# Expert selection cut into pieces, expert gates in full precision, input loaded ahead of the weights, and both norms of the first half pipelined on VectorE

## The chip, the cores and the metric

The kernel runs on one core of a Trainium2 chip. The metric is the device time of one execution in microseconds (us), the median of several runs. A core has five engines that run their own instruction streams and meet at semaphores: TensorE (PE) multiplies matrices, VectorE (DVE), ScalarE (ACT) and GpSimd (POOL) work on tiles in on-chip memory, and SyncE (SP) issues most transfers (DMAs). "PEld" is TensorE's loading of stationary operands.

## The reference

Two model halves run one after the other on 256 tokens of 2048 features, all in float32. Cut to what the change touches:

```python
# first half
h = rms_norm(x, mix_norm_g[l])            # first norm
proj = h @ w_in[l]                        # attention, an S5 scan and a gated merge follow
x = x + merged @ w_out[l]
h2 = rms_norm(x, ffn_norm_g[l])           # second norm
x = x + peer(h2, ...)                     # experts by product keys
# peer, for each of 256 tokens and 8 heads
q = (ht @ w_query).reshape(t_, PEER_HEADS, 2, PEER_HALF)
v1, i1 = lax.top_k(s1, 16)                # the 16 best of 128 keys, twice
v2, i2 = lax.top_k(s2, 16)
cand = v1[..., :, None] + v2[..., None, :]      # 256 sums of pairs
top_s, pos = lax.top_k(cand, 16)
idx = take_along_axis(cand_idx, pos, -1)  # 16 of 16384 experts
gate = jax.nn.softmax(top_s, axis=-1)
w = gate * gelu(u_sel . ht)               # u_sel: rows idx of expert_down
y = w @ v_sel                             # v_sel: rows idx of expert_up
```

The second half (a latent-attention layer and a grouped-query layer, with their norms) is not touched.

## The kernel before

**Products.** A float32 weight tile of 1 MB (128 rows x 2048) comes from HBM into a ring of slots. It is split into a high part `w_hi`, a rounded copy that TensorE takes as fp32r (ACT, `hi_split`, L371 to L380), and a remainder `w_lo = w - w_hi` (`lo_split`, L382 to L389, two halves of 1024 columns: half h = 0 and half h = 1). The activations are split alike into `h_hi` and `h_lo`. `dense` (L395 to L412) then does 16 blocks of three matmuls of 256 columns (hi x hi, lo x hi, hi x lo), 48 in all. It waits for `lo_done[1]` ahead of block 0 and for `lo_done[0]` ahead of block 8. As a rule POOL makes half 0 and DVE half 1. `w_hi` and `w_lo` are double, and a new `w_hi` waits until the tile two before is multiplied.

**Start.** SP issues the two halves of the input `X` (L453) and at once the weight tiles (L457), as many as there are free slots, seven at first. ACT's own queue brings vectors and constants (`vec`, `cst`), and ACT starts when they are in.

**Norms** (first norm ahead of the first weight tile, second norm ahead of the tiles `wq`). DVE takes a reciprocal (L1182) and makes `ht` in 16 steps, four to a quarter (L1185). ACT rounds each quarter to `h_hi` (L503). POOL subtracts for quarters 0 and 1 (`norm_lo`, L1017 to L1022), DVE for 2 and 3 (L1188 to L1193), after all 16 steps. TensorE waits for one quarter at blocks 0, 4, 8 and 12 of the first tile (`h_waits`, L1919).

**Stage "down0"** (64 weight tiles, `expert_down`): every token is multiplied with all 16384 experts, a tile giving 256 columns that ACT passes through GELU into `ab`. Meanwhile DVE selects experts (L1472 to L1490): for 8 heads and 2 token halves, 16 units in all, it makes 256 pair sums (L1480), takes the best 16 in two rounds (L1482, by `top16`), and looks up their two keys by comparing, multiplying and adding over 16 x 16 (L1486 to L1488). While DVE does that, in the first 4 * SELECT = 40 tiles, POOL makes both halves of `w_lo`. After tile 40 ACT waits for `sel_shifted`, takes the exponential of the selected scores (L697), DVE divides by the sums, and for the last 24 tiles DVE makes half 1 again.

**Stage "gates"** (32 groups of 8 tokens). TensorE turns the two keys and the weight so that the selected experts lie on partitions (L2117). DVE copies them to `kt` and `gp`, where `gp` is kept as a high and a low part (L1508, L1509). For each group DVE builds two one-hot tiles (`onehots`, L1525: `oh1` and `oh2`, shown in the trace by the buffers they live in, `w_lo` and `w_hi`). ACT multiplies `oh1` with the low part of the weights, eight tokens in eight instructions, and with the high part for the eighth (`gates_low`, L711 and L713). POOL does the high part of the other seven in one (`gates_high`, L1088). TensorE multiplies `oh2` by `g_hi` and by `g_lo` for each token (L2132, 16 fp32r matmuls of 128 columns), and the result, a 128 x 128 table of gates, is copied out by ACT (`gates_stage`, L722) and used by DVE to scale `ab` (L1531). A scaling of group n - 3 follows the one-hots of a group. Buffers are double.

**Order.** Every engine's order is as written in the code; loops `Fori` run on the engine.

## Time and profile before

| what | us |
|---|---|
| median of 3 runs | 4251.7 (4250.2 to 4260.3) |
| the profiled execution | 4263.7 |
| its span | 4261.7 |
| TensorE busy | 3990.8 (94%) |
| VectorE busy | 2483.0 (58%) |
| GpSimd busy | 1821.7 (43%) |
| ScalarE busy | 1667.3 (39%) |
| mean granted TensorE clock | 0.957 of full speed |

TensorE is busy nearly all the time, so work on another engine counts only where TensorE waits for it, or where TensorE runs at the lower of its two clocks. The chain of work that ended last goes through TensorE for 72% of the span, and through VectorE for 19%. The views that answer are those of single stretches (in a row of windows, "x" is the number of instructions, and the clock is the granted TensorE clock as a share of 2.4 GHz): the busy time by windows, the timeline, and the groups of one stage.

### The profile page before, as it was taken

The numbers are of one execution on the slowest core, as the hardware profiler recorded it, in microseconds if no ns is written. First come the engines' busy times: TensorE is split into PE (matmuls) and PEld (weight loads), VectorE is DVE, ScalarE is ACT, GpSimd is POOL, SyncE is SP. The second block draws the span as 40 slices with busy tenths as digits, with TensorE's granted clock in tenths as the row PEclk, the third lists the DMA queues.
The fourth block names the chain that finished last, engine by engine and source line by source line (L and its number), as shares of the span: only waits on it lengthen the run. The fifth ranks groups of instructions, "written<-read, shape, count | busy, mean of one in ns | idle before, by whom it ended". The sixth has DMA issues, their size and how long they took to land.

```text
span 4261.7 us, 73528 instructions
## 1 busy us (share of the span) xinstructions
PE 3990.8 (94%) x30180; PEld 3660.9 (86%) x30180; DVE 2483.0 (58%) x3055; ACT 1667.3 (39%) x2344; POOL 1821.7 (43%) x992
## 2 busy tenths in 40 slices
PE   7999998898998799999999999999999888979997
PEld 6776778798998799999999999999999556858877
DVE  5999965543799368777333577732221333657546
ACT  3222345543454466333444334422222122233574
POOL 4787843244487355444444444422222101233323
PEclk9999999999999876999999999999999899989999
DMA  5777763354555333555555555522222102213323
GB/s 203 307 298 293 276 242 134 117 192 159 178 188 177 130 126 107 187 187 187 215 213 204 193 190 178 185 101 99 98 98 91 58 30 99 89 60 138 119 91 137
DMA packets 132291, 679.30 MB, mean 159 GB/s; under 512 B 43665, under 2 KB 49937, under 8 KB 52369
## 3 DMA queue, kind: packets, MB, share of 16 engines
q1 hardware_dynamic: 89952, 641.77, 41.7%
q10 hardware_dynamic: 42160, 35.01, 2.5%
q8 instruction: 129, 2.11, 0.2%
q14 instruction: 50, 0.40, 0.0%
HBM read 664.15 MB, written 12.58 MB: 159 GB/s over the span
## 4 chain that ended last, share of the span: by engine, by line
PE 72%; DVE 19%; ACT 4%; issue 3%; POOL 1%; DMA 1%; DVEq 0%; ACTq 0%; POOLq 0%
PE banks L410 43%; PE banks L2150 16%; PE banks L2132 2%; PE banks L2270 1%; DVE w_lo L388 1%; DVE eq L1487 1%; DVE pq L1311 1%; PE banks L2062 1%; DVE banks L1301 1%; PE banks L2326 1%; ACT w_hi L380 1%; PE banks L2219 1%; DVE eq L1486 1%; DVE rq L1347 1%; PE banks L2218 1%
## 5 line engine op out<-in xcount | busy, mean ns | idle before, releaser
L388 POOL TENSOR_TENSOR w_lo<-ring,w_hi 128x1024 fp32r<-128x1024 f32 x533 | 1360.0, 2557 | 2224.2 <-ACT w_hi L380 2222.7
L410 PE MATMUL banks<-h_hi,w_hi 128*128 128x256 f32 (+1 forms) x6176 | 1660.2, 289 | 144.8 <-DVE w_lo L388 75.2
L410 PE MATMUL banks<-h_hi,w_lo 128*128 128x256 f32 (+1 forms) x6176 | 1637.4, 286 | 0.0
L410 PE MATMUL banks<-h_lo,w_hi 128*128 128x256 f32 (+1 forms) x6176 | 1637.2, 286 | 0.0
L380 ACT CAST w_hi<-ring 128x1024 fp32r<-128x1024 f32 x986 | 983.9, 1048 | 1065.5 <-PE banks L2150 459.0
L410 PEld LDWEIGHTS banks<-h_hi,w_hi 128*128 128x128 f32 x6176 | 1114.6, 190 | 215.8 <-issue 127.6
L410 PEld LDWEIGHTS banks<-h_lo,w_hi 128*128 128x128 f32 x6176 | 1117.8, 190 | 15.2
L410 PEld LDWEIGHTS banks<-h_hi,w_lo 128*128 128x128 f32 x6176 | 1114.3, 190 | 15.8 <-issue 0.5
L388 DVE TENSOR_TENSOR w_lo<-ring,w_hi 128x1024 fp32r<-128x1024 f32 x453 | 609.9, 1347 | 882.9 <-ACT w_hi L380 880.0
L2150 PE MATMUL banks<-wp_hi,w_hi 128*128 128x256 f32 x2048 | 577.0, 282 | 14.0 <-DVE wp_lo L1558 14.0
L2150 PE MATMUL banks<-wp_hi,w_lo 128*128 128x256 f32 x2048 | 575.1, 281 | 0.0
L2150 PE MATMUL banks<-wp_lo,w_hi 128*128 128x256 f32 x2048 | 575.1, 281 | 0.0
L2150 PEld LDWEIGHTS banks<-wp_hi,w_hi 128*128 128x128 f32 x2048 | 386.8, 189 | 16.4 <-issue 9.0
L2150 PEld LDWEIGHTS banks<-wp_lo,w_hi 128*128 128x128 f32 x2048 | 390.4, 191 | 0.0
L2150 PEld LDWEIGHTS banks<-wp_hi,w_lo 128*128 128x128 f32 x2048 | 388.2, 190 | 0.0
L1555 DVE TENSOR_SCALAR wp_hi<-ab 128x256 fp32r x128 | 314.3, 2456 | 0.7 <-DVE mods L1573 0.3
L683 ACT ACTIVATE ab<-banks 128x256 f32 (+1 forms) x128 | 49.3, 385 | 351.5 <-PE banks L410 351.4
L1042 POOL TENSOR_TENSOR cst<-tab 128x256 f32<-128x256 f32 x128 | 102.9, 804 | 73.6 <-DVE pq L1311 67.9
L2132 PE MATMUL banks<-g_hi,w_hi 128*128 128x128 f32 x256 | 107.2, 419 | 9.2 <-ACT g_hi L713 6.0
L2132 PE MATMUL banks<-g_lo,w_hi 128*128 128x128 f32 x256 | 106.3, 415 | 0.0
L1045 POOL TENSOR_TENSOR rot<-cst 128x256 f32<-128x256 f32 x128 | 97.8, 764 | 10.0
L1088 POOL TENSOR_TENSOR g_hi<-w_lo,gp 128x896 fp32r<-128x896 f32 x32 | 79.8, 2494 | 43.1 <-DVE w_lo L1525 43.1
(382 smaller groups left out, 4699.8 us busy)
## 6 DMA issues: line engine op xcount, KB each, us to landing
ring<-in_stream_dram SPq DMA_DIRECT2D x555, 1024.0 KB, 4.8
spare<-in_stream_dram SPq DMA_DIRECT2D x30, 1024.0 KB, 6.0
cst<-in_stream_dram SPq DMA_DIRECT2D x23, 1024.0 KB, 6.1
g_out<-stage ACTq DMA_DIRECT2D x32, 256.0 KB, 2.6
g_in<-g_out ACTq DMA_DIRECT2D x8, 1024.0 KB, 6.6
X<-in_x_in_dram SPq DMA_DIRECT2D x2, 1024.0 KB, 7.1
b_st<-in_ssm_b_dram ACTq DMA_DIRECT2D x8, 256.0 KB, 8.0
c_st<-in_ssm_c_dram ACTq DMA_DIRECT2D x8, 256.0 KB, 5.3
```

Source lines behind the costliest of these rows:

```text
L380: act.copy(w_hi[:, t.par, s], weights(t.slot)[:, s]).then_inc(hi_done, 1)
L388: eng.tensor_tensor(w_lo[:, t.par, s], weights(t.slot)[:, s], w_hi[:, t.par, s].bitcast(F32), ALU.subtract).then_inc(lo_done[h], 1)
L410: m = pe.matmul(bank(b, e - a, a), w[:, t.par, k], x(k)[:, a:e], start=first and a == 0, stop=last and e == n, skip_group_check=e - a < n)
L683: act.activation(ab[:, row], bank(t.bank(), T), ACT.Gelu).then_inc(acc_free[t.bank()], 1)
L1042: pool.tensor_tensor(rt[:, 0], A_(p0), B_(p1), ALU.mult)
L1045: pool.tensor_tensor(rot[:, u % 3, f], rt[:, 0], rt[:, 1], op).then_inc(S("rot_ready"), 1)
L1088: pool.tensor_tensor(g_hi[:, n % 2, 0:7], oh1[:, n % 2, 0:7].bitcast(F32), w, ALU.mult)\
L1301: m = dve.tensor_tensor_scan(scanned[:, z], dec, crossed[:, 1 - z], 0.0, ALU.mult, ALU.add)
L1311: m = dve.tensor_tensor(turned(u, pq[u % 3][:, f]), scanned, r[:, f:f + 1].to_broadcast([P, 2, T]), ALU.mult)
L1555: dve.tensor_scalar(wp_hi[:, j % 2], ab[:, i * 4 + j], 1.0, None, ALU.mult)\
L2132: m = pe.matmul(gate_banks(n)[:, t], oh2[:, n % 2, t], x[:, n % 2, t], start=(x is g_hi), stop=(x is g_lo))
L2150: m = pe.matmul(bank(k // 2, T, k % 2 * T), w[:, t.par, k], x[:, j % 2], start=(first and j == 0 and n == 0 and k % 2 == 0), stop=False, s ...
```

## The change

1. SP waits for the first half of `X` ahead of the first weight tile, and for the second half ahead of the second.
2. Both norms: POOL's part goes, and DVE makes all four `h_lo` quarters, quarter q - 1 behind the `ht` steps of quarter q. TensorE waits for DVE's count at all four places.
3. Selection: each of the 16 units is cut into three pieces (`pair_sums`, `second_half`, `keys_found`). One piece goes ahead of the two splits of a weight tile, tiles 4 to 51 of down0. DVE makes both halves of `w_lo` for all 64 tiles of down0, and POOL none. SELECT goes from 10 to 13: ACT takes the exponential after tile 52. The last two `sub_top` (L1455), which ran ahead of the loop, are spread over tiles 0 to 3.
4. Gates: `gp` is one float32 copy. ACT multiplies all eight tokens of `oh1` with it (eight instructions, `gw`), POOL does nothing, and TensorE does one full-precision matmul for each token in place of two fp32r ones.

The diff, cut to its core:

```diff
-SELECT = 10
+SELECT = 13
...
-        gp = place("gp", [P, 2, T], F32R, TA + 2 * K)
+        gp = place("gp", [P, T], F32, TA + 2 * K)
...
-        g_hi = place("g_hi", [P, 2, 8, P], F32R, TA + 4 * K)
-        g_lo = place("g_lo", [P, 2, 8, P], F32R, 64 * K + NVEC * 4 + CONST["nd"][0] * 4)
+        oh2 = place("oh2", [P, 2, 8, P], F32, 32 * K + idle * 8 * K)
+        oh1 = place("oh1", [P, 2, 8, P], F32, 48 * K + idle * 8 * K)
+        gw = place("gw", [P, 2, 8, P], F32, TA + 4 * K)
...
             for g in range(UNROLLED):
+                if g < 2:
+                    sp.wait_ge(S(f"x_in{g}"), 16)
...
                 for t in range(8):
-                    act.activation(g_lo[:, n % 2, t], oh1[:, n % 2, t].bitcast(F32), ACT.Copy,
-                                   scale=gp[:, 1, tokens(n, i, s, t, 1)].bitcast(F32))
-                act.activation(g_hi[:, n % 2, 7], oh1[:, n % 2, 7].bitcast(F32), ACT.Copy,
-                               scale=gp[:, 0, tokens(n, i, s, 7, 1)].bitcast(F32)).then_inc(S("g_lo_ready"), 1)
+                    m = act.activation(gw[:, n % 2, t], oh1[:, n % 2, t], ACT.Copy, scale=gp[:, tokens(n, i, s, t, 1)])
+                m.then_inc(S("gw_ready"), 1)
...
-            pool.wait_ge(lo_done[1], N0["down0"] + 1)
-            with pool.Fori(0, SELECT, 1) as i:
-                for j in range(4):
-                    for h in (1, 0):
-                        lo_split(pool, Tile("down0", j, i, 4).next(), h)
-            with pool.Fori(0, 16 - SELECT, 1) as i:
-                for j in range(4):
-                    lo_split(pool, Tile("down0", j, i, 4, skip=4 * SELECT).next(), 0)
-
-            def gates_high(n, i=None, s=0):
...
+            pool.wait_ge(lo_done[0], N0["up0"] + 1)
...
+            def norm(r, gain):
...
+                def low(q):
+                    c = slice(4 * q, 4 * q + 4)
+                    dve.wait_ge(S("h_hi_done"), 4 * r + q + 1)
+                    dve.tensor_tensor(h_lo[:, c], ht[:, c], h_hi[:, c].bitcast(F32), ALU.subtract)\
+                        .then_inc(S("h_dve"), 1)
+
                 for q in range(4):
                     for k in range(4 * q, 4 * q + 4):
                         m = dve.scalar_tensor_tensor(ht[:, k], X[:, k], V(gain, k), rs[:, 1], ALU.mult, ALU.mult)
                     m.then_inc(S("ht_ready"), 1)
+                    if q:
+                        low(q - 1)
+                low(3)
...
+            dve.wait_ge(lo_done[0], N0["down0"] + 1)
+            for n in range(64):
+                if n < 4:
+                    sub_top(14 + n // 2, n % 2)
+                elif n < 52:
+                    (pair_sums, second_half, keys_found)[(n - 4) % 3]((n - 4) // 6, (n - 4) // 3 % 2)
+                elif n == 53:
+                    weights_found()
+                if n == 51:
+                    dve.sem_inc(S("sel_shifted"), 1)
+                for h in (1, 0):
+                    lo_split(dve, Tile("down0", n).next(), h)
...
-            L(dve.tensor_copy(gp[:, 0], bank(6, T)))
-            L(dve.tensor_tensor(gp[:, 1], bank(6, T), gp[:, 0].bitcast(F32), ALU.subtract))
+            L(dve.tensor_copy(gp[:], bank(6, T)))
...
                 for t in range(8):
-                    for x in (g_hi, g_lo):
-                        m = pe.matmul(gate_banks(n)[:, t], oh2[:, n % 2, t], x[:, n % 2, t], start=(x is g_hi),
-                                      stop=(x is g_lo))
+                    m = pe.matmul(gate_banks(n)[:, t], oh2[:, n % 2, t], gw[:, n % 2, t], start=True, stop=True)
```

The order of VectorE's instructions in the first norm. Before:

```order
L1182 RECIPROCAL rs<-rs 128x256 [waits root,x_in1,x_in0]
L1185 SCALAR_TENSOR_TENSOR ht<-X,vec,rs 128x256 [waits dve_chain]
L1185 SCALAR_TENSOR_TENSOR ht<-X,vec,rs 128x256 x15
L1192 TENSOR_TENSOR h_lo<-ht,h_hi 128x1024 [waits h_hi_done] x2
L388 TENSOR_TENSOR w_lo<-ring,w_hi 128x1024 [waits hi_done]
```

The same place after the change (the lines of the `ht` steps and the subtraction are now L1162 and L1157):

```order
L1162 SCALAR_TENSOR_TENSOR ht<-X,vec,rs 128x256 x7
L1157 TENSOR_TENSOR h_lo<-ht,h_hi 128x1024 [waits h_hi_done]
L1162 SCALAR_TENSOR_TENSOR ht<-X,vec,rs 128x256 x4
L1157 TENSOR_TENSOR h_lo<-ht,h_hi 128x1024 [waits h_hi_done]
L1162 SCALAR_TENSOR_TENSOR ht<-X,vec,rs 128x256 x4
L1157 TENSOR_TENSOR h_lo<-ht,h_hi 128x1024 [waits h_hi_done] x2
L387 TENSOR_TENSOR w_lo<-ring,w_hi 128x1024 [waits hi_done]
```

The subtractions have moved in between the `ht` steps, and two of them are new here.

The order of VectorE's instructions in stage down0, at the start of a selection unit (`cand` holds the pair sums, `vv` and `ii` the best values and their places). Before:

```order
L1480 TENSOR_TENSOR cand<-tv 128x256 [waits dve_chain]
L1449 MAX vv<-cand 128x8 [waits dve_chain]
L1450 MAX_INDEX ii<-vv,cand 128x8 [waits dve_chain]
L1451 MATCH_REPLACE cand_101<-vv,cand 128x256
L1452 MAX vv<-cand_101 128x8 [waits dve_chain]
L1453 MAX_INDEX ii<-vv,cand_101 128x8 [waits dve_chain]
L1483 TENSOR_SCALAR ii<-ii 128x16 [waits dve_chain]
```

After:

```order
L1453 TENSOR_TENSOR cand<-tv 128x256
L1454 MAX vv<-cand 128x8 [waits dve_chain]
L1455 MAX_INDEX ii<-vv,cand 128x8 [waits dve_chain]
L1456 MATCH_REPLACE cand_101<-vv,cand 128x256
L387 TENSOR_TENSOR w_lo<-ring,w_hi 128x1024 [waits hi_done,dve_chain]
L387 TENSOR_TENSOR w_lo<-ring,w_hi 128x1024 [waits hi_done]
L1466 MAX vv<-cand_101 128x8
L1467 MAX_INDEX ii<-vv,cand_101 128x8 [waits dve_chain]
```

The two splits of the next weight tile now stand between the two rounds of a unit.

The order of TensorE's instructions at the first group of the gates. Before:

```order
L2132 MATMUL banks<-g_hi,w_hi 128x128 [waits kt_ready,g_lo_ready,g_hi_ready,oh2_ready]
L2132 MATMUL banks<-g_lo,w_hi 128x128
L2132 MATMUL banks<-g_hi,w_hi 128x128
L2132 MATMUL banks<-g_lo,w_hi 128x128
L2132 MATMUL banks<-g_hi,w_hi 128x128
```

After, where `oh_103` is `oh2`:

```order
L2126 MATMUL banks<-gw,oh_103 128x128 [waits kt_ready,gw_ready,oh2_ready]
L2126 MATMUL banks<-gw,oh_103 128x128 x7
L2126 MATMUL banks<-gw,oh_103 128x128 [waits gw_ready,oh2_ready]
L2126 MATMUL banks<-gw,oh_103 128x128 x7
L2126 MATMUL banks<-gw,oh_103 128x128 [waits gw_ready,oh2_ready]
```

Eight matmuls of a group stand where there were sixteen, and one semaphore takes the place of two.

## Rows read from the trace of the kernel before

**Rows 1.** Windows: start:end, length, busy (x) PE, PEld, DVE, ACT, POOL, clock, DMA, GB/s.

```profile
1544.40:1664.70 120.30, 116.58 (x512) 111.60 (x512) 116.05 (x93) 100.10 (x310) 77.32 (x31) 0.50 0.25 65
1375.30:1410.80 35.50, 0.00 (x0) 0.00 (x0) 31.35 (x97) 4.01 (x5) 0.26 (x1) 0.53 0.04 18
1410.80:1538.30 127.50, 127.47 (x1106) 127.47 (x1107) 28.20 (x23) 66.59 (x80) 59.54 (x24) 0.98 0.51 181
1145.80:1375.30 229.50, 225.99 (x1971) 223.99 (x1969) 222.93 (x246) 118.52 (x141) 195.22 (x80) 1.00 0.54 189
```

**Rows 2.** Timeline of ACT behind tile 40: start, length, instruction, [idle before <-releaser].

```profile
1406.74 0.42 ACT L697 ACTIVATE sv<-sv 128x256 f32<-128x256 f32 x1 [37.89 <-DVEq L1491]
```

**Rows 3.** Timeline of DVE in the selection: two units beside POOL, then one without.

```profile
1188.70 2.58 DVE L1480 TENSOR_TENSOR cand<-tv 128x256 f32<-128x256 f32 x1
...
1210.87 2.57 DVE L1480 TENSOR_TENSOR cand<-tv 128x256 f32<-128x256 f32 x1
...
1374.28 0.43 DVE L1480 TENSOR_TENSOR cand<-tv 128x256 f32<-128x256 f32 x1
...
1377.53 0.42 DVE L1486 TENSOR_TENSOR eq<-ii,cst 128x256 f32<-128x256 uint32 x1
...
1380.76 0.43 DVE L1480 TENSOR_TENSOR cand<-tv 128x256 f32<-128x256 f32 x1
```

**Rows 4.** Chain of waits at the end of down0: start, length, what.

```profile
1410.83 127.44 PE banks L410 x1104
```

**Rows 5.** Timeline of the first norm, all engines; the last row is the second norm's.

```profile
9.75 0.20 ACT L486 ACTIVATE small<-vec 128x1 f32<-128x1 f32 x1 [6.78 <-DMA cst<-in_consts_dram]
...
21.14 1.75 DVE L1182 RECIPROCAL rs<-rs 128x256 f32<-128x256 f32 x1 [0.73 <-ACT rs L482]
22.93 6.42 DVE L1185 SCALAR_TENSOR_TENSOR ht<-X,vec,rs 128x256 f32<-128x256 f32 x16
...
25.75 10.25 POOL L1021 TENSOR_TENSOR h_lo<-ht,h_hi 128x1024 fp32r<-128x1024 f32 x2 [3.15 <-ACT h_hi L503]
...
29.27 4.50 DVE L1192 TENSOR_TENSOR h_lo<-ht,h_hi 128x1024 fp32r<-128x1024 f32 x2
...
32.84 0.55 PE L410 MATMUL banks<-h_hi,w_hi 128*128 128x256 f32 x1 [12.34 <-POOL h_lo L1021]
...
1038.56 10.25 POOL L1021 TENSOR_TENSOR h_lo<-ht,h_hi 128x1024 fp32r<-128x1024 f32 x2 [8.16 <-ACT h_hi L503]
```

**Rows 6.** Windows, the first 9.75 us.

```profile
0.00:9.75 9.75, 0.00 (x0) 0.00 (x0) 0.00 (x0) 1.28 (x1) 0.20 (x4) 1.00 0.81 309
```

**Rows 7.** Tile X in the first 20 us: from issue to landing of its two halves.

```profile
DMA to landing us min/median/max: 5.9/7.1/8.3
```

**Rows 8.** Groups of DVE in gates, shapes kept apart: instructions, busy us, mean ns, idle before.

```profile
L1525 DVE TENSOR_TENSOR w_lo<-kt,cst 128x1024 fp32r<-128x1024 f32 x19 | 40.0, 2103 | 0.0
L1525 DVE TENSOR_TENSOR w_hi<-kt,cst 128x1024 fp32r<-128x1024 f32 x19 | 23.0, 1211 | 0.0
```

**Rows 9.** Timeline of one group of the gates on ACT, then on PE.

```profile
1590.51 2.16 ACT L711 ACTIVATE g_lo<-w_lo,gp 128x128 fp32r<-128x128 f32 x7 [0.51 <-DVE w_lo L1525]
...
1593.16 0.58 ACT L722 ACTIVATE stage<-banks 128x512 f32<-128x512 f32 x1
...
1589.66 0.45 PE L2132 MATMUL banks<-g_hi,w_hi 128*128 128x128 f32 x1
...
1592.89 0.41 PE L2132 MATMUL banks<-g_lo,w_hi 128*128 128x128 f32 x1
```

**Rows 10.** Chain of waits: two full-precision matmuls of 128 columns, in four records.

```profile
1138.81 0.44 PE banks L2100 x4
```

**Rows 11.** Windows with full-precision matmuls of 512 columns, then of 256 columns.

```profile
4135.30:4139.00 3.70, 3.53 (x8) 2.29 (x8) 0.06 (x1) 0.00 (x0) 0.00 (x0) 0.54 0.00 0
4139.00:4139.50 0.50, 0.00 (x0) 0.00 (x0) 0.37 (x1) 0.04 (x1) 0.00 (x0) 0.98 0.00 0
3382.00:3407.00 25.00, 25.00 (x32) 7.87 (x32) 5.04 (x10) 2.58 (x8) 0.00 (x0) 0.50 0.00 1
```

128 lines of the change are left out of this document (50 added, 78 removed).

## The prediction

> **What bounds the kernel now.** I read the busy shares first (TensorE 94%), then the windows of each stretch that the change touches, and in them what TensorE waits for. The reader should see three holes and one slow stretch.
>
> The largest hole is in the stage down0. TensorE is busy 226.0 of 229.5 us up to 1375.3, not at all for the next 35.5 us, and again for all of the last 127.5 us [rows 1]. The timeline says why: ACT stood idle 37.89 us until it took the exponential at 1406.74, and what released it was the end of the selection [rows 2]. ACT makes `w_hi`, so no tile could follow. VectorE did nothing but select in that time (222.9 of 229.5 us, then 31.35 of 35.5 [rows 1]). A unit of the selection, one head and one token half, took 1210.87 - 1188.70 = 22.17 us while POOL made both halves of `w_lo`, and 1380.76 - 1374.28 = 6.48 us when POOL had stopped [rows 3]. So the selection is late because POOL's splits stretch it more than threefold.
>
> The second and third holes are the norms. TensorE starts its first weight tile at 32.84, after 12.34 idle us, released by POOL's subtraction; POOL's two take 10.25 us beside VectorE's work, and the second norm has the same 10.25 [rows 5].
>
> The slow stretch is the gates: 120.3 us for 32 groups, 3.76 us each, TensorE busy 97% but at a granted clock of 0.50, that is 1.2 GHz [rows 1]. VectorE is the ring's bound: its groups show no idle time before them, and `oh1`, the first one-hot tile, takes 2103 ns where `oh2`, of equal size, takes 1211 [rows 8]. POOL runs beside the former: its 31 products are busy 77.32 us, 2.49 each [rows 1].
>
> **Part 1, down0.** A tile fed without a break costs: 127.44 us for 1104 records, which is 23 tiles of 48 [rows 4]; the clock was 0.98 over that window [rows 1], so about 2% of it, 2.5 us, was lost at its start, and 125.0 / 23 = 5.44 us a tile. Before, the 64 tiles took from 1145.84, TensorE's first matmul of the stage, to 1410.83 + 127.44 = 1538.27 [rows 4], together 392.4 us. After, VectorE does one piece and two splits a tile. A split alone costs 28.20 / 23 = 1.23 us [rows 1], two 2.45. The unit is 6.48 alone, a third 2.16; the longest piece, `keys_found`, is the stretch from the first comparison of keys at 1377.53 to the end of the unit, at most 1380.76 - 1377.53 = 3.23 [rows 3]. So VectorE needs 4.6 us a tile on average and 5.7 in the worst of three, against 5.44. The double `w_hi` and `w_lo` even out one tile by the next, and the third of 3.23 still holds the scores' subtraction, which moves to the shorter piece (0.27 us by its place in the unit, which leaves 2.96 and 5.4). TensorE stays fed: 64 x 5.44 = 348.2. I add 0.5 for the exponential after tile 52 with its two switches of ACT's function, between 0.3 and 2.5 (in the old place it and the splits behind it took 1410.83 - 1406.74 = 4.09 until TensorE ran [rows 2, 4], now with a tile in hand, so 4.09 less at least a part of 5.44). Gain 392.4 - 348.7 = 43.7, range 42 to 44.5. What hides the selection is TensorE's own 5.44 us a tile; without that cover a stalled VectorE costs its excess each tile (the rival below). The two copies moved into tiles 0 to 3 cost VectorE only. POOL's splits leave: 195.22 / 80 = 2.44 us each [rows 1], and nothing waits for POOL here.
>
> **Part 2, the norms.** Of the first norm, before: `ht` from 22.93, 0.40 a step, so quarters of 1.6 us; POOL begins 25.75, TensorE 32.84 [rows 5]. TensorE's second quarter starts 3.2 later (POOL's second subtraction ends at 25.75 + 10.25 = 36.0 [rows 5]), and 36 matmuls at 5.44 / 48 = 0.113 end tile 0 at about 40.2. After: two quarters of `ht` end at 22.93 + 3.21 = 26.14, `h_hi` of the first is there (POOL began on it at 25.75), a subtraction alone is a split alone in size, 1.23, so TensorE starts at 27.4. Then come quarter, subtraction, quarter, subtraction, subtraction: 1.6 + 1.2 + 1.6 + 1.2 + 1.2 = 6.8, so the last is there at 34.2, and TensorE, which needs 12 x 0.113 = 1.4 a quarter (2.6 at the lower clock), ends tile 0 at 35.6 to 36.8. Gain 4.5, between 3.5 and 5. The second norm has the same rows: 4.5 by this working, plus up to 0.6 because its tile 0 loses less at the lower clock if the clock has risen; I take 4.8, range 3.5 to 6. The other half of tile 1's `w_lo` was POOL's and stays POOL's, which is now free.
>
> **Part 3, the input first.** ACT, and with it the norm, starts at 9.75, when vectors and constants are in [rows 5]; the two halves of `X` took 5.9 and 8.3 us to land [rows 7]. In 9.75 us the queues moved 309 GB/s x 9.75 = 3.01 MB [rows 6]. `X` is 2.10 and vectors and constants 0.40, so 0.51 MB of weights went ahead. The engines of the queues were busy 0.81 of the time, so at full use they move 309 / 0.81 = 381 GB/s, and the weights took 1.3 us. Gain 1.0, between 0 (the constants wait for `X` instead) and 1.3. What is queued behind SP's new waits is the weight tiles; tile 0 lands later, but VectorE splits it only just ahead of the reciprocal at 21.14 [rows 5]. First norm and start together: 5.5, range 3.5 to 8.
>
> **Part 4, the gates.** POOL's product goes, so `oh1` should cost what `oh2` does: VectorE needs 3.76 - (2.10 - 1.21) = 2.87 a group [rows 1, 8]. ACT's ring is 1593.16 + 0.58 - 1590.51 = 3.23 with nine products [rows 9]; with eight it is 3.23 - 0.29 = 2.94 (one product is 2.16 less its overlap, by seven: about 0.29 [rows 9]). TensorE: the 16 records before go from 1589.66 to 1592.89, so 3.23 / 15 = 0.215 each and 3.44 a group at 1.2 GHz [rows 9]. A full-precision matmul of 128 columns took 0.44 / 2 = 0.22 in the stretch at full clock [rows 10], which is 0.44 at half: eight are 1.76 at 2.4 GHz and 3.44 to 3.52 at 1.2. So the number of matmuls halves and the work of TensorE does not. The pitch is 3.45 with TensorE as the bound if the clock stays, and that of ACT's ring plus handing over, 3.05 (2.94 to 3.2), if it rises. One copy and one product less ahead of the first group give 0.8 more.
> If it rises: 32 x (3.76 - 3.05) = 22.7, less 0.5 for the groups before it rises, plus 0.8: 23.0. If it stays: 32 x (3.76 - 3.43) + 0.8 = 11.4.
>
> **Which clock.** The rows speak both ways. Full-precision matmuls of 256 columns without a gap got the higher clock back after 3.7 us (0.54, then 0.98), and those of 512 columns did not in 25 us of unbroken work (0.50) [rows 11]. Before, the stage stayed at 0.50 with TensorE busy 97%, with a gap in each group [rows 1]. After, with TensorE as the bound at 1.2 GHz there would be no gap at all, and the matmuls are of the kind of the first row, with a weight load for each, as there (8 and 8), so I take the rise, with doubt.
> A page speaks to this. The Trainium skill, TensorE: Matmul & The Clock Gate, What's actually happening, says that the default state is throttled and that activity releases the throttle. By that rule the gates before, 97% busy, would stand at the higher clock already; the trace disagrees (0.50). The rule alone would give the rise for certain, 23.0 in the sum; the row of the stage alone gives 11.4.
>
> **Sum.** 43.7 + 4.8 + 5.5 + 23.0 = 77.0. The profiled execution took 4263.7 us and would take 4186.7; the median of the runs lies 12.0 below it, so 4174.7: **4175 us**.
>
> **The rivals.**
> A, forecast: all parts work and the clock rises in the gates: 4175, own range 4165 to 4181. Chance 0.58.
> B: all parts work, and TensorE at 1.2 GHz takes VectorE's place as the bound of the gates: 65.4 in all, 4186, own range 4181 to 4193. For it: 25 us without a gap at 0.50 [rows 11]. Chance 0.32.
> C, slower: a full-precision matmul of 128 columns costs four of the fp32r ones, 4 x 0.215 = 0.86 at 1.2 GHz. A group is then 6.9 us, 32 x 3.1 = 100 more than now instead of 23 less: 4251.7 - 54.0 + 100 = 4298. It decides against the change from 3.76 + 54.0 / 32 = 5.4 us a group. Against it: the four records of 0.44 in all [rows 10]. Chance 0.02.
> The Trainium skill, FP8 and Floating Point Precision, TensorE Precision Notes, gives four passes through the array for true FP32. With a pass priced at an fp32r matmul of 128 columns that is C; the trace agrees with the count only if such a matmul is itself no cheaper than one of 256 columns, and the sum by the row stays A or B.
> D, slower: the selection stays stretched though POOL is idle, because something else stretches it. A piece is then 22.17 / 3 = 7.4 and a tile 7.4 + 2.45 = 9.8 instead of 5.44: 48 x 4.4 = 211 more than in the sum: 4175 + 211 = 4386. It decides against the change from 77 / 48 = 1.6 us over 5.44 a tile. Against it: 6.48 as soon as POOL stopped [rows 3]. Chance 0.02, with another 0.01 for a mild form near no change.
> E: the start and the norms don't move (constants late, quarter by quarter handed over slower), the rest does: 77.0 - 10.3, or 65.4 - 10.3: 4185 to 4197. Chance 0.05.
>
> **How the numbers follow.** The likeliest is A. The range should hold 8 in 10: A with its own low end, 4165 (all terms at their best: 44.5 + 6 + 8 + 27 = 85.5), and B almost to its end, 4192. That leaves out C, D, part of E and B's last part. A measurement here can tell about 0.3%, 12.8 us. Faster by more is A, B and E, 0.95; slower C and D, 0.04; within 0.3% 0.01.
>
> **What would show it.** In down0: no idle TensorE between 1140 and the end of the stage, its length 349 us; VectorE's units in three pieces of 2 to 3 us, splits of 1.23. In the norms: TensorE's first matmul near 26.5 instead of 32.84, and some 5.3 earlier against the reciprocal in the second. In the gates: `oh1` at 1.21 us; pitch 3.05 at clock near 1.0, or 3.45 at 0.50. What would make the forecast wrong: splits slower than 1.23 beside the pieces, TensorE idle in every third tile (`keys_found`), or gates at 0.50.

## The result

| | us |
|---|---|
| before, median of 4 runs | 4256.0 (4250.2 to 4264.8) |
| changed, median of 4 runs | 4197.0 (4182.8 to 4205.5) |
| ratio | 0.986, 95% interval 0.984 to 0.988 |
| before, profiled execution (span) | 4263.7 (4261.7) |
| changed, profiled execution (span) | 4182.8 (4181.0) |

The kernel became faster, as forecast, by 59 us of 4256, where the forecast was 77. The 4197.0 lies 5 us above the end of the stated range. The two profiled executions are 80.9 us apart. So the traces and the medians tell two stories, and both have to be explained: whether the steps of the prediction were right, and why the first four runs show less.

Every record of a matmul keeps its number in TensorE's order (both traces hold 30180: a full-precision matmul leaves two records, so the gates have as many as before), and the starts of the same record can be compared. "The mark" is one such record, early in the first half of the model, at 96.6 us before and 94.2 after. The stages by these starts, in us:

| from the start of ... to ... | before | changed | difference |
|---|---|---|---|
| 0 to the first matmul of a weight tile | 32.8 | 27.9 | -4.9 |
| from there to the mark at 96 us | 63.8 | 66.3 | +2.5 |
| to a matmul in the last tile ahead of the second norm (1029) | 932.5 | 938.6 | +6.1 |
| from there to the first tile of `wq`, the second norm | 16.5 | 11.2 | -5.3 |
| `wq` | 100.2 | 97.3 | -2.9 |
| down0, to the turning of keys (L2117) | 392.1 | 348.9 | -43.2 |
| to the first matmul of the gates | 6.5 | 5.7 | -0.8 |
| gates, first to last matmul | 119.8 | 91.7 | -28.1 |
| to the end of up0 and down1 (2392) | 727.9 | 720.5 | -7.4 |
| the rest | 1850.9 | 1854.2 | +3.3 |

**Down0.** The windows of the changed kernel (columns as in [rows 1]): tiles 0 to 52, tiles 53 to 63, then the gates.

```profile
core 0: us, PE busy (x) PEld busy (x) DVE busy (x) ACT busy (x) POOL busy (x), PEclk, DMA share, GB/s
1141.50:1429.90 288.40, 288.37 (x2545) 288.17 (x2543) 220.66 (x441) 157.19 (x187) 0.00 (x0) 1.00 0.54 193
1430.40:1490.20 59.80, 59.80 (x527) 59.80 (x528) 28.18 (x27) 31.24 (x38) 0.00 (x0) 1.00 0.54 193
1495.90:1587.70 91.80, 66.83 (x511) 62.02 (x512) 87.76 (x92) 87.66 (x278) 0.00 (x0) 0.97 0.32 83
```

TensorE is busy for 288.37 of 288.40 us where [rows 1] had a hole of 35.5. Between the two windows lie 0.5 us: TensorE waits for what follows the exponential and its two switches of ACT's function. ACT's and TensorE's timelines there:

```profile
1424.97 1.28 ACT L698 ACT_TABLE_LOAD   x1
1426.27 0.42 ACT L698 ACTIVATE sv<-sv 128x256 f32<-128x256 f32 x1
1426.70 1.28 ACT L379 ACT_TABLE_LOAD   x1
1428.00 2.00 ACT L379 CAST w_hi<-ring 128x1024 fp32r<-128x1024 f32 x2
...
1430.36 0.38 PE L409 MATMUL banks<-h_hi,w_hi 128*128 128x256 f32 x1 [0.49 <-DVE w_lo L387]
```

From 1424.97 to 1430.36 the path is 5.39 us long, and the tile in hand hides all but 0.49 of it. ACT waited 37.89 for this exponential in [rows 2].

VectorE's timeline in the same stage, one tile with `second_half` and the split ahead of it:

```profile
1393.35 2.36 DVE L387 TENSOR_TENSOR w_lo<-ring,w_hi 128x1024 fp32r<-128x1024 f32 x2
1395.63 0.42 DVE L1466 MAX8 vv<-cand 128x8 f32<-128x256 f32 x1
...
1396.62 0.17 DVE L1468 TENSOR_SCALAR ii<-ii 128x16 uint32<-128x16 uint32 x1
...
1398.79 2.36 DVE L387 TENSOR_TENSOR w_lo<-ring,w_hi 128x1024 fp32r<-128x1024 f32 x2 [1.52 <-ACT w_hi L379]
```

Two splits take 2.36 and the piece 1.64 (1395.63 to 1397.27, the last step's end); VectorE then stands idle 1.52 and waits for ACT, the sign that it is not the bound.

**Gates.** Groups of the gates (columns as in [rows 8]):

```profile
L712 ACT ACTIVATE gw<-oh,gp 128x128 f32<-128x128 f32 x184 | 56.3, 400 | 0.1
L1521 DVE TENSOR_TENSOR oh<-kt,cst 128x1024 f32<-128x1024 f32 x46 | 54.3, 1216 | 0.1
L2126 PE MATMUL banks<-gw,oh 128*128 128x128 f32 x368 | 46.5, 280 | 19.0 <-ACT gw L712 19.0
```

The mean of both one-hots is 1216 ns, where `oh1` took 2103 [rows 8]; ACT and VectorE have 0.1 us of idle time in all before their instructions, TensorE 19.0. The clock is 0.97 of full over the stage where it was 0.50, with 66.83 us of TensorE work in place of 116.58 [rows 1]. A group takes 91.8 / 32 = 2.87 us.

**Norms.** The first norm in the changed kernel, VectorE and TensorE, up to the third weight tile:

```profile
9.65 0.20 ACT L487 ACTIVATE small<-vec 128x1 f32<-128x1 f32 x1 [6.67 <-DMA cst<-in_consts_dram]
...
21.56 1.75 DVE L1152 RECIPROCAL rs<-rs 128x256 f32<-128x256 f32 x1 [0.73 <-ACT rs L483]
23.35 3.25 DVE L1162 SCALAR_TENSOR_TENSOR ht<-X,vec,rs 128x256 f32<-128x256 f32 x8
26.52 1.22 DVE L1157 TENSOR_TENSOR h_lo<-ht,h_hi 128x1024 fp32r<-128x1024 f32 x1
...
27.88 0.55 PE L409 MATMUL banks<-h_hi,w_hi 128*128 128x256 f32 x1 [6.97 <-DVE h_lo L1157]
...
42.56 1.21 DVE L387 TENSOR_TENSOR w_lo<-ring,w_hi 128x1024 fp32r<-128x1024 f32 x1
...
43.92 0.50 PE L409 MATMUL banks<-h_hi,w_hi 128*128 128x256 f32 x1 [2.02 <-DVE w_lo L387]
```

From reciprocal to TensorE it is 27.88 - 21.56 = 6.32 us, against 32.84 - 21.14 = 11.70 in [rows 5], 5.4 less. But ACT began at 9.65 against 9.75: the input ahead of the weights brought a tenth of a microsecond. At 43.92 TensorE waits 2.02 us for VectorE. Before, the same matmul waited 0.75:

```profile
46.67 0.36 PE L410 MATMUL banks<-h_hi,w_hi 128*128 128x256 f32 x1 [0.75 <-DVE w_lo L388]
```

Behind the wait of 2.02 the granted clock fell, to 0.76 over this tile of the changed kernel:

```profile
43.90:51.10 7.20, 7.18 (x49) 7.20 (x50) 3.61 (x4) 1.83 (x4) 2.37 (x1) 0.76 0.29 124
```

The second norm has no such wait behind it:

```profile
1037.63 1.75 DVE L1152 RECIPROCAL rs<-rs 128x256 f32<-128x256 f32 x1 [1.84 <-ACT rs L483]
...
1043.96 0.55 PE L409 MATMUL banks<-h_hi,w_hi 128*128 128x256 f32 x1 [6.96 <-DVE h_lo L1157]
```

That is 6.33 us again.

**What no part of the change explains.** Two windows of 50 us in down1, first of the kernel before, then of the changed kernel:

```profile
2168.00:2218.00 50.00, 50.00 (x427) 50.00 (x426) 16.68 (x12) 19.64 (x28) 26.13 (x9) 1.00 0.57 208
```

```profile
2090.00:2140.00 50.00, 50.00 (x444) 50.00 (x443) 17.33 (x12) 21.18 (x29) 25.87 (x9) 1.00 0.58 210
```

The code is the same, TensorE is busy all the time and its clock is granted in full in both, yet it does 427 matmuls in one and 444 in the other. The starts of neighbouring matmuls lie 117.8 ns apart in the first and 113.3 in the second. These are the two distances of its dense work of 256 columns at full clock, and long stretches have the one or the other. Counted over blocks of 24 matmuls, the kernel before had 1312 us at 117.8 ns and the changed one 991. The longer distance costs 1 - 113.3 / 117.8 = 3.8% of the time spent in it, so these two traces differ by 12 us for a reason that is none of the four parts. A second such reason, time at the lower clock in stretches that the change does not touch, stands at the end of the experiments. TensorE's timeline of the changed kernel where the one passes into the other:

```profile
2051.19 0.28 PE L409 MATMUL banks<-h_hi,w_lo 128*128 128x256 f32 x1
2051.31 0.28 PE L409 MATMUL banks<-h_lo,w_hi 128*128 128x256 f32 x1
2052.03 0.38 PE L409 MATMUL banks<-h_hi,w_hi 128*128 128x256 f32 x1 [0.44 <-DVE w_lo L387]
...
2052.61 0.28 PE L409 MATMUL banks<-h_hi,w_lo 128*128 128x256 f32 x1
2052.72 0.28 PE L409 MATMUL banks<-h_lo,w_hi 128*128 128x256 f32 x1
```

Steps of 0.12 before, steps of 0.11 behind a pause (0.7 us between two starts) in which TensorE waited 0.44 us for a split.

### The profile page after: what moved, and what is told of

It is laid out like the page before. It is cut to its first block, busy times and chain, and to the rows that moved or that the text cites. A ratio compares the mean times of both kernels' runs of the same rounds, so it can differ in the third digit from the quotient of the medians.

```text
span 4181.0 us, 73152 instructions
## 1 busy us (share of the span) xinstructions
PE 3937.4 (94%) x30180; PEld 3612.0 (86%) x30180; DVE 2419.1 (58%) x3162; ACT 1655.5 (40%) x2312; POOL 1461.6 (35%) x852
## 4 chain that ended last, share of the span: by engine, by line
PE 76%; DVE 14%; ACT 4%; issue 3%; POOL 1%; DMA 1%; ACTq 0%; DVEq 0%; POOLq 0%
PE banks L409 49%; PE banks L2143 16%; DVE w_lo L387 2%; PE banks L2263 1%; PE banks L2057 1%; DVE pq L1283 1%; DVE banks L1273 1%; PE banks L2319 1%; ACT w_hi L379 1%; PE banks L2212 1%; ACT gw L712 1%; DVE rq L1319 1%; PE banks L2211 1%; DVE banks L1260 1%; PE banks L2385 1%
## 5 line engine op out<-in xcount | busy, mean ns | idle before, releaser
L387 POOL TENSOR_TENSOR w_lo<-ring,w_hi 128x1024 fp32r<-128x1024 f32 x429 | 1098.4, 2561 | 2557.3 <-ACT w_hi L379 2555.8
L387 DVE TENSOR_TENSOR w_lo<-ring,w_hi 128x1024 fp32r<-128x1024 f32 x557 | 730.2, 1321 | 860.7 <-ACT w_hi L379 857.3
L1033 POOL TENSOR_TENSOR cst<-tab 128x256 f32<-128x256 f32 x128 | 105.8, 826 | 73.1 <-DVE pq L1283 67.4
L1036 POOL TENSOR_TENSOR rot<-cst 128x256 f32<-128x256 f32 x128 | 97.3, 760 | 10.0
L2126 PE MATMUL banks<-gw,oh 128*128 128x128 f32 x512 | 67.1, 287 | 29.7 <-ACT gw L712 29.7
L1034 POOL TENSOR_TENSOR cst<-tab 128x256 f32<-128x256 f32 x128 | 93.7, 732 | 0.0
L2126 PEld LDWEIGHTS banks<-gw,oh 128*128 128x128 f32 x512 | 62.1, 199 | 34.8 <-issue 34.8
```

Source lines behind the costliest of these rows:

```text
L387: eng.tensor_tensor(w_lo[:, t.par, s], weights(t.slot)[:, s], w_hi[:, t.par, s].bitcast(F32), ALU.subtract).then_inc(lo_done[h], 1)
L1033: pool.tensor_tensor(rt[:, 0], A_(p0), B_(p1), ALU.mult)
L1034: pool.tensor_tensor(rt[:, 1], A_(p2), B_(p3), ALU.mult).then_inc(S("rt_ready"), 1)
L1036: pool.tensor_tensor(rot[:, u % 3, f], rt[:, 0], rt[:, 1], op).then_inc(S("rot_ready"), 1)
L2126: m = pe.matmul(gate_banks(n)[:, t], oh2[:, n % 2, t], gw[:, n % 2, t], start=True, stop=True)
```

## The experiments

My theory: the terms of the sum are right but for the start of the kernel, and the medians are shifted by the two distances of TensorE's matmuls, drawn anew in each execution. Rivals: the gates get the higher clock in some executions only; the parts need each other; other waits changed.

### The changed kernel again, twice

No edit.

> The changed kernel once more, unaltered. Its profiled execution was 4182.8 us, its median 4197.0, and the terms worked out before add up to the profiled one. In both traces TensorE's full-clock matmuls of 256 columns follow each other at one of two distances, 113.3 ns or 117.8 ns, in long stretches that change only where TensorE pauses: 1312 us of the kernel before and 991 us of the changed one lie in the longer distance. Theory: what is missing from the sum is this, and it is drawn anew in each execution. Then this profile shows another length of the 117.8 ns stretches, and its time differs from 4182.8 by 3.8% of the difference of these lengths (100 us more of them: 3.8 us more), with every stage that the change touches as long as before to 1 us (down0 348.8, gates 91.7 from first to last matmul). Rival: the gates stay at half clock in the slower executions; then the gates last 110 us there and the granted clock is near 0.96. Second rival: waits for weights differ; then idle TensorE between the stages differs by 10 us.

Measured: median 4182.3 us (4177.2 to 4184.5, 5 runs), ratio 0.982 (0.980 to 0.984); profiled 4177.2, with 822 us at 117.8 ns. Down0 348.9, gates 92.2. Against the first trace: 169 us less at 117.8, so 6.4 us forecast, 5.6 measured.

> The changed kernel a third time. The first four executions had a median of 4197.0 us, the next five 4182.3. If both are draws of one distribution that the length of the 117.8 ns stretches sets, the median here lies between 4180 and 4200, and this profile's time against the two profiled before (4182.8 us with 991 us at 117.8 ns, 4177.2 with 822) follows 3.8% of the difference of these lengths to 3 us. If the first four had another cause, time and length part by more than 5 us.

Measured: median 4179.2 us (4172.7 to 4183.5, 5 runs), ratio 0.984 (0.982 to 0.986); profiled 4172.7, 746 us at 117.8 ns. Against the first trace 245 us less, 9.3 us forecast, 10.1 measured; the median fell just below the interval I gave. Down0 348.9 and gates 91.9 once more, and the granted clock was 0.971 or more in all 14 executions, so the gates never fell back to half clock (110 us at 0.50 would make it 0.96). The first rival falls for the gates. The 14 executions of the changed kernel have a median of 4182.5 (4172.7 to 4205.5). Those of the kernel before, 53 in all, have 4257.6 (4237.5 to 4283.4). The difference is 75.0 us. The three runs at 4191.9 to 4205.5 are all from the first four and have no trace; a longer share at 117.8 ns is the likely cause, since a later variant with 1583 us of it took 4213, and their mean granted clocks, 0.974 to 0.976, are as high as those of the faster executions, which speaks against time at the lower clock. For these three it is not shown.

### Each part alone on the kernel before

The edits are the diff's pieces: selection with down0's splits; gates; input and norms.

> Part 3 of the change alone on the kernel before: selection in pieces, both halves of w_lo on VectorE in down0, exponential after tile 52. Forecast by the working: down0 from 392.4 to 348.7 us, so 43.7 us less; nothing else moves but the stretches of the longer matmul distance. If the selection were fast only together with the other parts, less than 40.

```profile
1142.70:1491.60 348.90, 348.41 (x3074) 348.21 (x3073) 249.56 (x469) 189.01 (x225) 0.00 (x0) 1.00 0.53 193
```

Measured: 4217.4 us (4212.2 to 4229.3, 4 runs), ratio 0.991 (0.988 to 0.994); the window is down0, 348.9 us, TensorE idle 0.49.

> Part 4 alone on the kernel before: gates by one full-precision matmul a token, no POOL product. The changed kernel had the 32 groups at 2.96 us each. Forecast: the same here, stage from 119.8 to about 92 us between first and last matmul, 28 us less in all. If the clock rises only because of the state in which the new down0 leaves TensorE, it stays at 0.50 here, with 3.45 a group and 10 us less.

```profile
1540.00:1632.00 92.00, 66.76 (x511) 62.08 (x512) 87.74 (x92) 87.63 (x278) 0.00 (x0) 0.97 0.32 83
```

Measured: 4225.5 us (4219.2 to 4249.5, 7 runs), ratio 0.994 (0.991 to 0.997); the window is the gates at clock 0.97. The clock rises without the new down0.

> Parts 1 and 2 alone on the kernel before: input ahead of the weights, both norms on VectorE. The changed kernel's first matmul of a weight tile came 5.0 us earlier, but the lead had shrunk to 1.6 us at 61 us, and after the second norm it won 5.6. Forecast by the working 10.3 together; by the trace of the changed kernel 2 + 5.5, 7.5. Theory: what shrinks the lead is the chain of small VectorE steps ahead of the third tile's split; then this profile shows it too, at the same place.

Measured: 4246.1 us (4234.1 to 4259.9, 10 runs), ratio 0.997 (0.995 to 0.999). TensorE starts at 27.7, and 93.1 instead of 96.6 at the mark; the second norm takes 11.2 instead of 16.5. 3.5 + 5.3 = 8.8, between the two forecasts. The wait for the third tile is there too, 2.15 us.

Against the median of the kernel before, taken beside them (4257.2), the three are 39.7, 31.7 and 11.1 us lower, together 82.5, against 74.9 for the whole change run beside them: within the spread of the runs the parts add up, and none needs another.

### Is it the pieces or POOL's leaving?

```diff
-                for h in (1, 0):
-                    lo_split(dve, Tile("down0", n).next(), h)
+                lo_split(dve, Tile("down0", n).next(), 1)
...
+            with pool.Fori(0, 16, 1) as i:
+                for j in range(4):
+                    lo_split(pool, Tile("down0", j, i, 4).next(), 0)
```

> The changed kernel, with POOL making the first half of w_lo in down0 as in all other stages, and VectorE the second half and the pieces. It tells whether the pieces or POOL's leaving brought the 43 us. If the pieces: a piece and one split fit into 5.44 us also beside POOL, and down0 stays at 349 us. If POOL's leaving: pieces stretch while POOL works (2.5 of each 5.44 us), VectorE needs up to 2.2 + 2.5 + 1.2 = 5.9 us a tile in 48 tiles, and down0 takes 349 + 48 x 0.5 = 370 us or more.

VectorE's timeline of one piece, `keys_found`, and the window of down0:

```profile
1303.99 1.23 DVE L387 TENSOR_TENSOR w_lo<-ring,w_hi 128x1024 fp32r<-128x1024 f32 x1 [1.20 <-ACT w_hi L379]
1305.14 2.62 DVE L1462 TENSOR_TENSOR eq<-ii,cst 128x256 f32<-128x256 uint32 x1
...
1308.71 0.43 DVE L1462 TENSOR_TENSOR eq<-ii,cst 128x256 f32<-128x256 uint32 x1
...
1312.46 1.23 DVE L387 TENSOR_TENSOR w_lo<-ring,w_hi 128x1024 fp32r<-128x1024 f32 x1
```

```profile
1134.00:1504.00 370.00, 357.61 (x3069) 355.82 (x3068) 270.15 (x404) 188.99 (x225) 164.93 (x64) 0.99 0.50 182
```

Measured: 4192.4 us (one run), down0 370.6 us, 21.7 more than without POOL, under 3 of it from the longer distance of matmuls; TensorE is idle for 12.4 us of the window instead of 0.5. In this piece the same comparison takes 2.62 us while POOL subtracts (from 1304.92 to 1307.48) and 0.43 without, and the piece 7.3 instead of 3. The time agrees with the working that priced it (5.9 us a tile, 370). So of the 43 us, half remains when POOL makes one half of each `w_lo`, and the other half comes when POOL makes none. POOL made both halves before, so the first half of the gain is that of the pieces, of the later exponential and of the POOL work already gone, and what the pieces bring beside POOL's full share is not shown.

### What raised the clock of the gates?

Two kernels. In the first POOL multiplies again, into a buffer that nothing reads:

```diff
+            with pool.Fori(0, 16, 1) as i:
+                for n in range(2):
+                    product(n, i, 2)
...
                     dve.wait_ge(S("gw_ready"), g(-1))
+                    dve.wait_ge(S("product"), g(-1))
```

> The changed kernel, with POOL multiplying one-hots and weights in the gates as before, into a buffer that nothing reads; the next one-hots wait for it. The full-precision matmuls stay. VectorE's one-hots should go back to 2.1 us, a group to 3.76 us, and TensorE should have the gaps of the kernel before at half clock (3.4 of 3.76 us). It tells the clock apart: if the unbroken TensorE work is what brought the full clock, it stays at 0.50 here; if the kind of matmul is, it rises to 1.0 though a group lasts 3.76. Either way the stage is about 28 us longer than in the changed kernel, which says that VectorE beside POOL was the bound and not TensorE.

In the second POOL stays away, and the matmuls are fp32r again:

```diff
-                    m = pe.matmul(gate_banks(n)[:, t], oh2[:, n % 2, t], gw[:, n % 2, t], start=True, stop=True)
+                    for x in range(2):
+                        m = pe.matmul(gate_banks(n)[:, t], oh2[:, n % 2, t], gw[:, n % 2, t], start=x == 0, stop=x == 1)
```

> The changed kernel, with the gates multiplied by two rounded (fp32r) matmuls a token, as before the change, both with the same weighted one-hots; the low part of the weights is left out, and the output is not the reference's. ACT, VectorE and POOL are as in the changed kernel. It prices the precision alone. If the kind of matmul is what raised the clock (POOL's product put back left it at full), it stays at 0.50 here, TensorE is the bound at 3.45 us a group, and the stage takes 109 us instead of 92. If the absence of POOL's product did it, the stage stays at 92 us and the clock at 1.0.

The gates' windows, of the first kernel and of the second:

```profile
1487.00:1605.20 118.20, 69.82 (x511) 64.54 (x512) 116.11 (x93) 90.21 (x278) 77.29 (x31) 0.95 0.25 65
```

```profile
1492.00:1600.80 108.80, 108.80 (x511) 108.80 (x512) 89.97 (x92) 90.46 (x278) 0.00 (x0) 0.50 0.27 71
```

With POOL's product (one run, 4209.3 us) the stage takes 118.3 us at clock 0.95, 26.5 more than the changed kernel, and TensorE is busy only 69.82 of 118.2; a group is back at 3.76 us. With fp32r (one run, 4200.3 us; this kernel leaves out the low part of the weights) it takes 109.0 at 0.50, TensorE busy all the time. So the kind of matmul decides about the clock here and the gaps do not: fp32r matmuls of 128 columns stay at half clock at 100% busy, full-precision ones of 128 columns get the full clock at 59%. Of the two reasons in the prediction, no gap and the kind of matmul, only the second holds. fp32r alone is not what keeps the clock down: right behind the gates, the changed kernel's fp32r matmuls of 256 columns begin at 0.50 and stand at 1.00 in the second row:

```profile
1591.50:1596.50 5.00, 5.00 (x24) 5.00 (x25) 1.78 (x2) 1.99 (x2) 0.79 (x1) 0.50 0.91 243
1597.10:1607.10 10.00, 10.00 (x89) 9.90 (x88) 6.60 (x6) 3.96 (x4) 3.58 (x2) 1.00 0.36 116
```

The higher clock alone brings next to nothing (118.3 against 119.8), POOL's leaving alone 10.8, both together 28.1.

### The start

> The changed kernel without part 1: weights are issued right behind the input again. Forecast before: first matmul of a weight tile 1.0 us later than the 27.9 of the changed kernel. The traces since: ACT began at 9.65 instead of 9.75, so the waits gained 0.1 us at most; then it stays at 27.4 to 28.0.

```profile
9.36 0.20 ACT L485 ACTIVATE small<-vec 128x1 f32<-128x1 f32 x1 [6.38 <-DMA cst<-in_consts_dram]
```

Measured (edit: SP's two waits taken out): 4182.1 us (one run); ACT begins at 9.36, TensorE at 27.2, 91.9 at the mark instead of 94.2. In the ten traces with the waits ACT begins at 9.35 to 9.91, TensorE at 27.0 to 28.0, and the mark lies at 92.5 to 94.8. Part 1 gains nothing that shows; what releases ACT is the constants, and they don't land sooner. The next kernel asks where half of the norm's gain went:

```diff
                 lo_split(dve, t.next(), 1)
+                if j == 1:
+                    decay()
...
-                if j == 0:
-                    decay()
```

> The changed kernel, with VectorE's chain of ten small steps for the scan's decay moved behind the split of the third tile instead of ahead of it. In the changed kernel that split starts at 42.56 us, behind the chain, TensorE waits 2.0 us for it, and of 5.0 us won at the first tile 2.4 are left at 96 us. Theory (the chain is what takes the gain back): TensorE's wait there goes and 4 to 4.5 us are left at 96 us. Rival (ACT's two table switches ahead of the high part are as late): the lead stays near 2.4.

VectorE and TensorE in that kernel:

```profile
38.23 1.23 DVE L387 TENSOR_TENSOR w_lo<-ring,w_hi 128x1024 fp32r<-128x1024 f32 x1 [2.41 <-ACT w_hi L379]
39.37 2.43 DVE L1119 TENSOR_TENSOR s5w<-vec,s5w 128x64 f32<-128x64 f32 x1
...
43.04 2.38 DVE L1125 TENSOR_SCALAR s5w<-s5w 128x64 f32<-128x64 f32 x1
...
47.16 1.22 DVE L387 TENSOR_TENSOR w_lo<-ring,w_hi 128x1024 fp32r<-128x1024 f32 x1
```

Measured: 4195.0 us (one run). The third tile's split starts at 38.23 instead of 42.56 and TensorE's wait for it is gone. But two steps of the chain now stretch to 2.4 us instead of 0.2 (in the changed kernel one did), the fourth tile's split is late at 47.16, TensorE waits 2.3 us for it, and from its first tile to the mark it is 66.4 us, in the changed kernel 66.3. Neither theory nor rival as I put them: the chain is the cause of the wait, and moving it moves the wait. How much the wait costs up to the mark also hangs on the clock: five of the ten traces whose start has the changed kernel's order of VectorE's work fell to half clock behind it and needed 66.3 to 66.9 us, the others, at full clock, 64.7 to 65.3.

### Can the shorter distance be had on purpose?

First two pauses, at tiles 11 and 31 of up0, each in a tile that stands outside the loop:

```diff
+                    if j == 3 and skip in PAUSE[half]:
+                        pe.wait_ge(hi_done, 2 * t.next().n0 + 1)
```

> The changed kernel, with two pauses of TensorE put into the first expert-up stage: ahead of its tiles 11 and 31 TensorE waits until the first half of the next tile's high part is there, about 1.3 us each. In the two traces of the changed kernel the distance of the matmuls goes from 113.3 to 117.8 ns within the first six tiles of this stage and stays there for 385 and 435 us, until a pause of 0.72 us comes by itself. In the six traces so far the longer distance ended at 22 of 27 pauses of 0.7 us or more. Theory (the distance is set anew by a pause and by nothing else): after the first or the second pause the stage runs at 113.3 ns, the longer distance lasts under 180 us here, and the stage up to the next one is 8 to 14 us shorter than 716.5, less 2.6 for the pauses. Rival (the distance belongs to the place in the program, or to the heat or power drawn): it comes back within a few tiles, and the kernel is 3 us slower.

TensorE at the first of them, and windows before it, behind it and two tiles on:

```profile
1664.91 0.28 PE L2147 MATMUL banks<-wp_hi,w_lo 128*128 128x256 f32 x1
1665.03 0.28 PE L2147 MATMUL banks<-wp_lo,w_hi 128*128 128x256 f32 x1
1666.44 0.39 PE L2147 MATMUL banks<-wp_hi,w_hi 128*128 128x256 f32 x1 [1.13 <-ACT w_hi L379]
```

```profile
1650.00:1664.00 14.00, 14.00 (x122) 14.00 (x121) 10.81 (x8) 4.38 (x5) 7.19 (x3) 1.00 0.60 221
1667.00:1677.00 10.00, 10.00 (x91) 10.00 (x90) 7.16 (x6) 2.35 (x3) 4.98 (x2) 1.00 0.51 198
1680.00:1694.00 14.00, 14.00 (x121) 14.00 (x120) 10.66 (x8) 4.00 (x4) 7.17 (x3) 1.00 0.59 207
```

8.7, 9.1 and 8.6 matmuls a microsecond (a window also counts those that reach into it): both pauses brought 113.3 ns, and both times it was 117.8 again 97 matmuls later, after a lag (one start that comes 0.1 us late). Median 4186.8 (4176.9 to 4213.2, 6 runs), ratio 0.984 (0.981 to 0.987); no gain. The profiled execution is the slowest, 4213.2, with 1583 us at 117.8 ns: there down0 too had fallen into it and took 362.3 instead of 348.9.

Then one pause in each up stage, in the loop's first turn, on the thought that the lag comes from entering the loop:

```diff
+                    if j == 3 and skip == 4:
+                        pe.wait_ge(hi_done, 2 * Tile(f"up{half}", 3, skip=4).next().n0 + 1)
```

> The changed kernel, with one pause of TensorE of about 1.3 us in each of the two expert-up stages, at the fourth tile of the loop's first turn (a wait for a constant count, so that it holds in the first turn only). The two pauses tried before did bring the distance of the matmuls from 117.8 back to 113.3 ns, and it went up again two tiles later, at a lag of 0.1 us in the first turn of the loop entered anew. In all traces that lag comes in a loop's first turn. Theory: behind the first turn nothing lags, so the stage stays at 113.3 ns; up to the next stage it takes 696 to 704 us instead of 716 to 725, the longer distance lasts under 600 us in all, and the median is 10 to 20 us below the changed kernel's 4184. Rival (the longer distance belongs to the place): back within some tiles, 2.6 us slower.

Measured: 4190.3 us (4187.3 to 4202.2, 6 runs), ratio 0.983 (0.980 to 0.986); up0 and down1 720.1 us from their first matmul, where the three traces of the changed kernel have 716.1 to 718.8; 896 us at 117.8 ns. In the first of the two stages 113.3 ns held for four tiles behind the pause, with a lag of 0.1 us after two and after four, and the second lag ended it, inside the loop; in the other stage the lag after two tiles ended it. So the lags follow the pause itself and not the entry. My thought falls, and with it the gain. That a pause can end the longer distance is shown four times on purpose; a way to keep the short one was not found. Nor does a pause always bring the short one. Counted where 12 matmuls on either side follow each other evenly, in the six traces read first (before, changed twice, and the three parts), the longer distance ended at 23 of 26 pauses (0.7 us or more between two starts), and the shorter at 20 of 57, the pause at 46.67 us of the kernel before among these. (The expectation above has 22 of 27, by another count.)

**A second thing that differs from execution to execution.** The profiled execution of this kernel took 4194.2 us, 11.4 more than the first of the changed kernel, though its share at 117.8 ns is 95 us shorter. Its two pauses, 1.69 us between two starts each, cost about 3 us, and the rest lies in the second half of the model, which no kernel here touches. Windows of the same records there, of the changed kernel and of the one without part 1:

```profile
3395.30:3433.70 38.40, 34.09 (x121) 18.67 (x120) 13.69 (x27) 11.07 (x30) 0.00 (x0) 1.00 0.08 28
```

```profile
3384.30:3433.80 49.50, 45.19 (x121) 22.67 (x120) 13.79 (x26) 11.04 (x30) 0.00 (x0) 0.76 0.06 22
```

In both TensorE has waited 2.78 us just ahead, and only in the second the granted clock then falls. Nine of the fourteen traces have 38.4 us and clock 1.00 here, five (those without part 1, with POOL's product, with the decay chain moved, and the two with pauses) 49.5 to 54.0 and 0.76 to 0.68. So single runs of these five can't be compared with those of the others by their totals; the readings above rest on single stages. The attention stage, from 689 to 846 us before, has the same cause of spread:

```profile
689.10:846.20 157.10, 133.12 (x963) 122.61 (x962) 85.12 (x162) 87.94 (x156) 39.25 (x16) 0.96 0.33 114
```

```profile
687.10:849.70 162.60, 138.38 (x963) 128.25 (x962) 85.08 (x162) 87.91 (x156) 39.27 (x16) 0.93 0.31 111
```

The work is the same, the clock is 0.96 before and 0.93 in the changed kernel. Over all fourteen traces this stage is the longer the lower its clock (to 0.3 us), from 154.7 us at 0.98 to 162.7 at 0.93. What decides whether the clock falls behind a pause, stays open.

## Why the prediction was right or wrong

**The forecast time, 4175, range to 4192: too low for the four runs, by 5 us at the range's end.** The step that failed is the last of the sum: I carried the 12.0 us between the profiled execution and the median of three runs over as if it were fixed, and gave the range no width for the runs themselves. Both medians move. Over all its executions the kernel before stands at 4257.6, not 4251.7, and the changed one at 4182.5. The forecast difference, 77.0, is close to the measured 75.0; a base of 4257.6 would have given 4180.6. So the 22.3 us between 4174.7 and 4197.0 are 5.9 of base, 1.9 of the terms together, and 14.5 by which the first four executions lay above the median of all fourteen. That the terms together are off by so little is in part luck, since the start fell short and the gates gave more. The spread of one execution is 33 us for the changed kernel and 46 for the one before, and a median of four can be off by 15.

**Down0, 43.7:** measured 43.2 in the profiled pair and 43.2 with the part alone (392.1 to 348.9). The 0.5 for the exponential was 0.49. The worst case of 5.4 for `keys_found` did not show as idle TensorE. That POOL's work stretches VectorE's is shown by POOL's half put back, which costs 21.7.

**Norms:** TensorE's start behind the reciprocal, 5.4 us earlier where the working gave 5.4 (32.84 to 27.4). In the second norm 5.3 of 4.8 forecast. In the first, the step that failed is the one that asked what is late next: I followed tile 0 to its end and tile 1's split, and stopped one tile short. Tile 2's split stands behind VectorE's ten decay steps, which wait for ACT's two function switches. TensorE's wait for it grew from 0.75 to 2.02, and behind it the clock fell to 0.76 for that tile: 2.4 left of 4.9 at 96 us.

**Input first, 1.0:** nothing, and the low end of the range was the right one. The step that failed took the bytes that had moved ahead of the constants as the cause of their landing time. Without the waits ACT began at 9.36, with them at 9.65, and at 9.35 to 9.91 over all traces that have them.

**Gates, 23.0:** measured 28.9, which is 28.1 in the stage and the 0.8 ahead of it that the term held. Two terms of A were mis-sized: a group takes 2.81 to 2.87 instead of 3.05, since little is added for handing over, and the 0.5 for the groups before the clock rises does not show. B did not come about, but its price, TensorE as the bound at 0.50, can be read from the fp32r kernel: 109.0 us for the stage, 10.8 less than before, where 10.6 had been reckoned beside the 0.8. Of the reasons for the rise, no gap was not the condition, and the kind of matmul was. The rows that I took the rise from were thin: the first two of [rows 11] are those of 256 columns (its heading has the order the other way round), and in the second, at 0.98, TensorE does nothing. The Trainium skill, TensorE: Matmul & The Clock Gate, What's actually happening, would have the clock released by activity; the fp32r window shows 108.80 us of unbroken work at 0.50, so here the trace disagrees with busy time as the measure of activity.

**Rivals C and D:** a group keeps TensorE busy for 2.09 us at nearly full clock (66.83 for 32 groups), where C needs half of 6.9; the pieces did not stay stretched. E is true for the start in part.

**Not in the sum at all:** 12 us between the two profiled traces from the distance of matmuls, with up0 and down1 faster by 7.4 and `wq` by 2.9; and 6.1 us lost between the mark at 96 us and the second norm, 5.5 of them in the attention stage from 689 to 846 us. That stage took 157.2 before, 162.7, 159.3 and 162.5 in the three traces of the changed kernel, and 154.7 to 160.9 in its variants with the same code there, by the granted clock in it. It is not a cost of the change: in the other two traces of the changed kernel the whole way from the mark to the second norm is 0.9 and 0.6 us shorter than before. That the profiled pair differed by 80.9, near the forecast, is in part luck: 79.8 come from the parts (2.4 + 5.3 + 43.2 + 28.9), and the 12 gained by the distance and the 6.1 lost are two draws.

## What to carry to other kernels

Price a second engine's work by what it does to the first: in down0 half of the gain came only when the last of POOL's splits had gone, and the faster matmuls of the gates were worth little until POOL had gone. When a start is moved forward, follow the pipeline until a tile is fed as before, two or three tiles past the first, and name each engine's queue on the way. Take the spread of single executions into a range before the terms, and compare stages by the starts of the same instruction rather than by totals; where a stage that nobody changed differs, look at its granted clock first.

## What the runs showed of the hardware

TensorE's dense fp32r matmuls of 256 columns at full granted clock have two distances, 113.3 and 117.8 ns (444 against 427 in 50 us), each kept over up to some 700 us. Within rows of these matmuls alone the distance changed only at pauses or lags of TensorE, but for two places in fourteen traces (at 2602 us with POOL's product in the gates, at 2652 in the first kernel with pauses). In six traces the longer ended at 23 of 26 pauses and the shorter at 20 of 57. Why, stays open.

The clock behind a pause: after the same wait of 2.78 us, the same matmuls got the full clock throughout in nine traces (38.4 us) and fell to half in five (49.5 to 54.0 us).

Matmuls of 128 columns: two fp32r ones took 0.43 us at half clock [rows 9] and one in full precision 0.22 at full clock [rows 10], by the clock about as many cycles, but only the latter brought the full clock in this stage, at 59% busy, while the former stayed at 0.50 at 100%. At half clock an fp32r matmul took 0.213 us at 128 columns (the fp32r kernel, 109.0 us for 512) and at 256 (the changed kernel, 24 in the 5.00 us from 1591.50): at 128 columns two fp32r matmuls saved TensorE nothing against one in full precision.
